# Products of a mixer's output matrix divided by rows of the array, two halves side by side

## The reference, cut to what matters

```
def hybrid_mixer(h, w_in, ..., w_br, w_out, lambda_init):
    ...
    merged = (gates[:, :, 0] * (ya @ w_br[0]) + gates[:, :, 1] * (yb @ w_br[1])
              + gates[:, :, 2] * (yc @ w_br[2]))
    return merged @ w_out          # merged: 512 x 1024, w_out: 1024 x 1024

x = x + hybrid_mixer(rms_norm(x, norm_mix_g[l]), w_in[l], ...)
```

## Time and profile before

| | us |
|---|---|
| median of two runs | 1765.04 (1764.94 to 1765.14) |
| the profiled execution, its own time | 1765.09 |
| its span (first to last instruction) | 1763.3 |
| TensorE products, busy | 1754.0 (99%), 8152 of them |
| TensorE weight loads, busy | 1453.1 (82%) |
| VectorE busy | 1244.3 (71%) |
| ScalarE busy | 730.7 (41%) |
| GpSimd busy | 483.6 (27%) |

### The profile page before, as it was taken

One profiled execution on the slowest core, in us unless ns is written; L12 is line 12 of the kernel. 1 busy time (PEld: TensorE's weight loads), 2 busy tenths in 40 slices (PEclk: granted clock), 3 DMA queues, 4 the chain that ended last, 5 costly groups with the idle time before them and its releaser, 6 DMA issues.

```text
span 1763.3 us, 21613 instructions
## 1 busy us (share of the span) xinstructions
PE 1754.0 (99%) x8152; PEld 1453.1 (82%) x8152; DVE 1244.3 (71%) x1656; ACT 730.7 (41%) x940; POOL 483.6 (27%) x201
## 2 busy tenths in 40 slices
PE   9999999999999999999999999999999999999998
PEld 7888888888878888888878888888888788888888
DVE  7987856563568776577779678555744797685586
ACT  5233644343464433343432346443444544343342
POOL 6453000103014244444133620010030232444440
PEclk9999999999999999999999999999999999999999
DMA  5532222322222322232332313223222223322322
GB/s 216 190 120 72 102 102 84 132 95 96 96 96 96 120 101 91 97 117 80 114 143 72 143 62 109 105 93 123 96 96 96 96 96 120 114 78 96 120 74 70
DMA packets 30120, 185.95 MB, mean 105 GB/s; under 512 B 3644, under 2 KB 5948, under 8 KB 9536
## 3 DMA queue, kind: packets, MB, share of 16 engines
q1 hardware_dynamic: 27804, 172.71, 27.6%
q0 software_dynamic: 1648, 11.54, 1.7%
q10 hardware_dynamic: 564, 0.33, 0.1%
HBM read 179.25 MB, written 7.68 MB: 106 GB/s over the span
## 4 chain that ended last, share of the span: by engine, by line
PE 98%; DVE 0%; DMA 0%; ACT 0%; issue 0%; POOL 0%; SPq 0%; DVEq 0%; ACTq 0%; POOLq 0%
PE ps L1531 28%; PE ps L1532 28%; PE ps L1541 28%; PE ps L1447 2%; PE ps L1438 2%; PE ps L1439 2%; PE ps L1569 1%; PE ps L1589 1%; PE ps L1621 1%; PE ps L1603 1%; PE ps L1581 0%; PE ps L1701 0%; PE ps L1702 0%; PE ps L1708 0%; DMA resid<-x_t 0%; PE ps L1552 0%
## 5 line engine op out<-in xcount | busy, mean ns | idle before, releaser
L1531 PE MATMUL ps<-x_hd,w_hd 128*128 128x512 f32 x1584 | 619.3, 391 | 0.0
L1532 PE MATMUL ps<-x_tl,w_hd 128*128 128x512 f32 x1584 | 616.7, 389 | 0.0
L547 POOL TENSOR_TENSOR w_tl<-raw,w_hd 128x2048 fp32r<-128x2048 f32 x80 | 370.0, 4624 | 536.1 <-ACT w_hd L652 397.3
L652 ACT ACTIVATE w_hd<-raw 128x2048 fp32r<-128x2048 f32 (+1 forms) x156 | 298.4, 1913 | 344.8 <-PE ps L1532 260.4
L1541 PE MATMUL ps<-x_hd,w_tl 128*128 128x512 f32 x1584 | 377.3, 389 | 0.0
L1531 PEld LDWEIGHTS ps<-x_hd,w_hd 128*128 128x128 f32 x1584 | 297.4, 188 | 62.7 <-issue 0.3
L1532 PEld LDWEIGHTS ps<-x_tl,w_hd 128*128 128x128 f32 x1584 | 297.4, 188 | 61.2
L1541 PEld LDWEIGHTS ps<-x_hd,w_tl 128*128 128x128 f32 x1584 | 297.0, 188 | 61.6
L1531 PE MATMUL ps<-ring_hd,w_hd 128*128 128x512 f32 (+1 forms) x640 | 242.0, 382 | 0.0
L1532 PE MATMUL ps<-ring_tl,w_hd 128*128 128x512 f32 (+1 forms) x640 | 239.8, 379 | 0.0
L900 DVE TENSOR_TENSOR w_tl<-raw,w_hd 128x2048 fp32r<-128x2048 f32 x75 | 171.9, 2293 | 51.5 <-ACT w_hd L652 40.1
(11 more groups left out here) (198 smaller groups left out, 1524.0 us busy)
## 6 DMA issues: line engine op xcount, KB each, us to landing
raw<-units SPq DMA_DIRECT2D x155, 1024.0 KB, 4.8
resid<-x_t SPq DMA_DIRECT2D x4, 512.0 KB, 8.0
bias_t<-bias_tiles POOLq DMA_DIRECT2D x8, 256.0 KB, 5.1
cg<-mem_t POOLq DMA_DIRECT2D x2, 1024.0 KB, 6.1
resid<-x_t POOLq DMA_DIRECT2D x1, 2048.0 KB, 8.3
resid_dram<-resid POOLq DMA_DIRECT2D x1, 2048.0 KB, 7.7
resid<-resid_dram POOLq DMA_DIRECT2D x1, 2048.0 KB, 8.9
out<-resid SPq DMA_DIRECT2D x7, 256.0 KB, 2.4
```

Source lines behind the costliest of these rows:

```text
L547: line.done(pool.tensor_tensor(w_tl[:, k % 2, :], raw[:, k % 2, :], w_hd[:, k % 2, :].bitcast(F32), ALU.subtract), of_unit("tail", g))
L652: line.done(act.activation(out, in_, func, **kw), *labels)
L1531: pe.matmul(dst, w_hd[:, slot, w], hd[:, src, :], start=kc == 0, stop=False)
L1532: i = pe.matmul(dst, w_hd[:, slot, w], tl[:, src, :], start=False, stop=False)
```

## The change

For the kind "out" alone, `product` gets an order of its own. Each product of 128 rows is divided into two of 64 rows (`rows_pair`). In `turn` 0 the upper half of the array (partitions 0 to 63) works for output tile 0 and the lower half for output tile 1; in `turn` 1 it is the other way round. So each output tile gets both halves of its contraction, one in each turn, and the halves never write one bank at the same time. The order is: turn 0 with `w_hd`, turn 1 with `w_hd`, turn 1 with `w_tl`, turn 0 with `w_tl`. At each change of turn TensorE waits for its own semaphore, so that the last products of one turn have landed before the other half adds to the same bank. The `mg_tail` waits stand together ahead of the first product.

```
+                if kind == "out":
+                    for kc in range(nk if tag else 0):
+                        pe.wait_ge(vector_done, line.at(f"{tag}_tail{kc}"))
+
+                    def rows_pair(turn, kc, weights, moving, first, last):
+                        for r in (0, 1):
+                            w, src, dst = block(kc, turn if r == 0 else 1 - turn)
+                            rows = slice(64 * r, 64 * r + 64)
+                            i = pe.matmul(dst, weights[rows, slot, w], moving[rows, src, :], start=first, stop=last)
+                        return i
+
+                    for kc in range(nk):
+                        rows_pair(0, kc, w_hd, hd, kc == 0, False)
+                        i = rows_pair(0, kc, w_hd, tl, False, False)
+                    line.done(i, f"rows_0_{unit}")
+                    pe.wait_ge(tensor_done, line.at(f"rows_0_{unit}"))
+                    for kc in range(nk):
+                        rows_pair(1, kc, w_hd, hd, False, False)
+                        i = rows_pair(1, kc, w_hd, tl, False, False)
+                    line.done(i, of_unit("used", unit))
+                    tails_ready(unit)
+                    for kc in range(nk):
+                        i = rows_pair(1, kc, w_tl, hd, False, False)
+                    line.done(i, f"rows_1_{unit}")
+                    pe.wait_ge(tensor_done, line.at(f"rows_1_{unit}"))
+                    for kc in range(nk):
+                        i = rows_pair(0, kc, w_tl, hd, False, kc == nk - 1)
+                    return i
```

## The result

| | before | changed |
|---|---|---|
| median of two runs, us | 1765.04 | 1784.84 (1784.42 to 1785.25) |
| the profiled execution, its own time | 1765.09 | 1785.25 |
| its span | 1763.3 | 1783.5 |
| TensorE products, records | 8152 | 8536 |
| granted clock, mean | 0.998 | 0.996 |

The ratio is 1.0112, with a 95% interval from 1.0095 to 1.0128: 20 us longer, and within 2%. The forecast was 1785.

What follows compares the result with a forecast made beforehand. TensorE was taken to bound the kernel, busy 99% of the span. Terms of 0 + 10.0 + 5.8 + 0.4 + 4.0 = +20.2 us on 1765.1 gave 1785.3 us, range 1774 to 1792.

Steps and rivals of the forecast that it cites:

- products in pairs: Out units: 384 pairs of 64-row products cost what 384 full products cost, 226.6 ns each, so 0 us.
- moved waits: First out product of each layer now waits for VectorE's last activation tail: +5.1 us in layer 0, +4.9 in layer 1.
- 16 waits for itself: Two per out unit, at changes of turn: drain, answer and uncovered load lose 0.36 us each, 5.8 us in all.
- leaving the halves: Behind each layer's fourth out unit, passing from half to full height loses 0.2 us, twice: +0.4 us.
- clock: The 5 us stop ahead of each layer's out units drops the clock, 2.0 us lost each time: +4.0 us.
- four float32 records: Attention products of 64 rows, two on each half: 1.13 us for four, read as halves running side by side.
- the constant of 13.4 ns: Time per 512-column product beyond one column per cycle at 2.4 GHz; forecast to stay in pairs.
- The rival of the faster pairs: Out units: the constant per product goes in pairs, saving 5.1 us, for 1780 us; chance 0.24.
- The rival of no overlap: Out units: halves don't run side by side, each pair costs two products, +87 us, 1872 us; chance 0.10.
- the 3.2 of the earlier trace: End of the trace before: clock fell 3.2 us after products became sparse, so a 5 us stop should lower it.
- the 5.0 of the start: Start of the trace before: 5.0 us of work at the lower level before the clock rose, 2.5 us lost.

Runs made afterwards that it cites:

- pairs alone: Kernel before, with pairs only in the last three out units of each layer, lower half in banks of its own, no waits of TensorE for itself: 1765.77 us.
- a lone half: Kernel before, with only the upper half's 64-row products in the last three out units of each layer, output lacking the lower half's part: 1765.74 us.
- pairs of 256 columns: Changed kernel with every half product divided once more into two of 256 columns: 1789.74 us.
- half after half: Changed kernel with each block's list reordered, all upper-half products first, then all lower-half ones, instead of alternately: 1857.04 us.

## Why the prediction was right

The sum, term by term, in us:

| term | predicted | shown by |
|---|---|---|
| products in pairs | 0 | 0: pairs alone, 1765.77 with the passing in it |
| moved waits | 5.1 + 4.9 | 5.2 + 4.95 in the trace |
| 16 waits for itself | 5.8 (0.36 each) | 5.9 (0.37 each in the trace); 0.33 to 0.38 in three runs |
| leaving the halves | 0.4 | 0.4 (0.2 each), won back right behind |
| clock | 4.0 | 3.6 (2.0 + 1.6) |
| sum | 20.2 | 20.05; the medians differ by 19.80, the profiled executions by 20.16 |

By the traces the two "out" stretches, from the last product of unit 31 to the second product behind unit 35, are longer by 10.4 and 9.8 us, 20.2 together, against 20.05 of the terms. That the whole differs by nearly the same is in part chance. The 0.4 us won back behind the stretches was not in the forecast. The profiled execution of the changed kernel was also 0.45 us late before its first "out" unit, where nothing had been changed; the run with the moved waits alone was 0.03 us late there.

- *Pairs.* That the halves run side by side was read from four float32 records, and it held in float32r, where each column goes in once. That the constant of 13.4 ns stays in each half held too: it is there in a lone half, and in pairs of 256 columns. The rival of the faster pairs falls. The rival of no overlap falls as well; something near it came only with the list reordered. The Trainium skill (TensorE: Matmul & The Clock Gate, Back-to-back issue gap) gives about 216 ns as the isolated distance for 512 columns; neither pairs nor full products met it here, at 227 ns.
- *The moved waits.* Read to 0.1 us from two rows, and it is the largest term. The run with this edit alone, 1778.78, gives the stop and the clock together as 13.6 us; the table has 10.15 + 3.6 = 13.75.
- *Waits for itself.* Built from a drain, an answer and a load, it came out at 0.36. The trace of after has the last pair's start at 0.45 us ahead of the next load, 0.02 to 0.03 less than the 0.48 that I had put together, and some unevenness in the next few pairs that makes up for it.
- *Leaving the halves.* The border costs 0.195 us, as read from the earlier trace rows, where a release by ScalarE might have had a part. The way in costs the same and was hidden by the stop, as said. What the term left out is that the next product which had waited for VectorE takes the 0.2 us up again, so over the whole program it is worth nearly nothing.
- *The clock.* The fall in both layers came as forecast, and the price 0.4 us below it. The comparison behind it was looser than I wrote: in layer 0 the clock fell 2.6 us after the last product, less than the 3.2 of the earlier trace rows, and in layer 1 only as the products came back, 4.9 us after the last one. So in layer 1 that it fell at all was partly luck, though it did so in all seven kernels whose stop is not filled. And the time to the rise was 4.3 and 3.4 us of dense work, not the 5.0 of the start. The two losses of 2.0 and 1.6 lie inside my bounds of 0 and 2.5.

The change gives nothing back: no product is shorter, and none of the runs with halves is faster than the kernel before.

## What to carry to other kernels

Where a matrix already fills the array's 128 rows, two halves side by side took the time of one full product (227 ns), so the division is judged by the waits that it brings. Whether the waits for itself are needed for a right sum is not shown: no run lets both halves write one bank without them. Look first at where an edit moves waits for an input's pieces: here 13.6 of 20 us came from waits gathered ahead of a loop that had hidden them, and the clock behind the two stops of 5 us added 3.6 to their 10.2. If TensorE must stand that long, products into a bank that is cleared next can keep the clock: they did so ahead of pairs, and in three of four stretches ahead of lone halves.

## What the runs showed of the hardware that I had not expected

- Products of 64 rows alone kept a clock that was up (32.5 us at 1.00 behind full-height work) but did not raise one that had fallen: 81.5 us without a gap at 0.50, then a rise some 5 us into full-height work. Pairs raised it in 3.4 and 4.3 us, and with half after half, where only some products run side by side, it took 25 and 26 us.
- The constant per product is a matter of the upper level. At 1.2 GHz products of 512 columns are 427 ns apart, full and half height alike, which is the columns alone; at 2.4 GHz they are 226.7 apart, 13.4 more than the columns.
- The two products of a pair start 2 to 4 ns apart in most of the changed kernel (33 or 62 at 1.2 GHz, and mostly 16 to 24 in the run without the waits for itself), and one half's products can start ahead of up to three of the other half's that the list has before them.
- TensorE's wait for its own semaphore costs 0.33 to 0.38 us, and passing from 128 rows to 64 or back 0.195 us.
